# Expert units of 32 rows on four 32-column tiles in a mixture-of-experts stage

## What is computed

```python
def moe_ffn(h, w_router, b_router, w_gate_up, b_gate_up, w_down, b_down):
    ...
    top_logit, top_idx = lax.top_k(logits, TOP_K)      # 4 of 32 experts for each of 512 tokens
    top_w = jax.nn.softmax(top_logit, axis=-1)
    ...
    def expert_block(args):
        xe, e = args
        gu = xe @ w_gate_up[e] + b_gate_up[e]          # 1024 -> 2048
        gate = jnp.minimum(gu[:, :D_FF], SWIGLU_LIMIT)
        up = jnp.clip(gu[:, D_FF:], -SWIGLU_LIMIT, SWIGLU_LIMIT)
        act = (up + 1.0) * gate * jax.nn.sigmoid(SWIGLU_ALPHA * gate)
        return act @ w_down[e] + b_down[e]             # 1024 -> 1024
```

## Time and profile before

| | |
|---|---|
| time, 3 runs | 3245.38 us median, 3240.45 to 3245.57 |
| profiled execution | 3247.26 us, its span 3245.4 us |
| TensorE busy | 3111.7 us, 96% of the span |
| VectorE, ScalarE, GpSimd busy | 1361.0, 806.4, 388.4 us |
| granted TensorE clock, mean | 0.989 |
| moved by DMA | 632.90 MB |

### The profile page before, as it was taken

One profiled execution on the slowest core, in us unless ns is written; L12 is line 12 of the kernel. 1 busy time (PEld: TensorE's weight loads), 2 busy tenths in 40 slices (PEclk: granted clock), 3 DMA queues, 4 the chain that ended last, 5 costly groups with the idle time before them and its releaser, 6 DMA issues.

```text
span 3245.4 us, 41103 instructions
## 1 busy us (share of the span) xinstructions
PE 3111.7 (96%) x14106; PEld 1838.5 (57%) x14107; DVE 1361.0 (42%) x2096; ACT 806.4 (25%) x1573; POOL 388.4 (12%) x314
## 2 busy tenths in 40 slices
PE   7999899989999999999999999999999999999999
PEld 5555555464788633333333333333787888888887
DVE  2475555664345412121212121212467577554542
ACT  3343343420211211111111111111325355311100
POOL 0132221331000000000000000000301354000000
PEclk9999999999999999999999999999899999999999
DMA  5313142236312599999999997797412121222121
GB/s 222 117 72 130 59 143 97 98 152 229 128 52 106 203 348 394 381 386 383 389 393 388 380 390 279 304 364 275 154 52 95 59 72 49 88 91 78 65 78 56
DMA packets 190025, 632.90 MB, mean 195 GB/s; under 512 B 18752, under 2 KB 56000, under 8 KB 179168
## 3 DMA queue, kind: packets, MB, share of 16 engines
q1 hardware_dynamic: 161216, 552.79, 44.5%
q0 software_dynamic: 10944, 39.85, 3.4%
q10 hardware_dynamic: 17760, 38.78, 3.4%
HBM read 594.78 MB, written 36.57 MB: 195 GB/s over the span
## 4 chain that ended last, share of the span: by engine, by line
PE 78%; issue 7%; DMA 5%; DVE 4%; POOL 2%; ACT 2%; SPq 1%; ACTq 0%; DVEq 0%; POOLq 0%
PE ps L323 24%; PE ps L2325 17%; PE ps L2299 11%; PE ps L2016 7%; PE ps L272 6%; DMA slot<-in_w_exp 5%; PE ps L2554 2%; PE ps L2068 1%; POOL decay L3409 1%; PE ps L2526 1%; PE ps L2509 1%; PE ps L2294 1%; SPq L1358 1%; POOL x_dt L3398 1%; PE ps L1945 1%
## 5 line engine op out<-in xcount | busy, mean ns | idle before, releaser
L2325 PE MATMUL ps<-slot,xT_blk 128*64 128x512 f32 x3200 | 736.1, 601 | 28.7 <-DMA slot<-in_w_exp 26.4
L2325 PEld LDWEIGHTS ps<-slot,xT_blk 128*64 128x64 f32 x3200 | 219.0, 137 | 466.7 <-issue 378.0
L2299 PE MATMUL ps<-slot,aT 128*64 128x512 f32 x1632 | 362.8, 597 | 0.9 <-ACT aT L1706 0.9
L2016 PE MATMUL ps<-hT,slot 128*128 128x512 f32 (+1 forms) x896 | 309.5, 504 | 7.4 <-DVE xT L2734 6.3
L3065 DVE TENSOR_TENSOR gate<-ps,b_row 128x512 f32<-128x512 f32 x50 | 34.5, 691 | 520.2 <-PE ps L2325 520.1
L2299 PEld LDWEIGHTS ps<-slot,aT 128*64 128x64 f32 x1632 | 117.4, 137 | 237.9 <-issue 237.9
L2016 PEld LDWEIGHTS ps<-hT,slot 128*128 128x128 f32 x896 | 169.0, 191 | 136.7 <-issue 121.2
L2684 DVE SCALAR_TENSOR_TENSOR conv<-ps,g_conv,conv 128x510 f32<-128x510 f32 (+1 forms) x224 | 133.3, 631 | 178.5 <-ACT conv L1500 175.1
L3061 DVE MEMSET b_there<- 128x1 f32 x50 | 3.0, 59 | 386.5 <-DMA b_few<-in_b_gu 379.2
L1681 ACT ACTIVATE y_row<-ps 128x512 f32<-128x512 f32 x51 | 30.4, 597 | 383.9 <-PE ps L2299 383.9
L323 PE MATMUL ps<-in_t,in_s 128*128 128x264 f32 x528 | 124.8, 386 | 0.5 <-issue 0.5
(11 more groups left out here) (510 smaller groups left out, 4688.0 us busy)
## 6 DMA issues: line engine op xcount, KB each, us to landing
slot<-in_w_exp SPq DMA_DIRECT2D x768, 512.0 KB, 9.1
in_w<-in_w_ffn SPq DMA_DIRECT2D x22, 1024.0 KB, 4.8
expert_rows<-zero SPq DMA_DIRECT2D x4, 4608.0 KB, 22.4
slot<-in_w_xbc SPq DMA_DIRECT2D x8, 2048.0 KB, 7.7
sum_here<-sum_rows ACTq DMA_DIRECT2D x32, 512.0 KB, 3.6
w_modT<-in_w_modT POOLq DMA_DIRECT2D x32, 512.0 KB, 3.6
rnn_w<-in_w_rnn SPq DMA_DIRECT2D x16, 1024.0 KB, 4.8
expert_rows<-y_row ACTq DMA_DIRECT2D x102, 128.0 KB, 5.6
```

Of the source, the lines that this page charges most:

```text
L2016: last = pe.matmul(ps[:, 2 * (m % 2) + part, 0:n], w[:, (k * 4 + m % 4) * P:(k * 4 + m % 4 + 1) * P], hT[:, k, c0:c0 + n], start=(k == 0), ...
L2299: last = pe.matmul(ps[h * UNIT:(h + 1) * UNIT, 6, :], aT[:, t, d * UNIT:(d + 1) * UNIT], slot[4 + d][:, t * D + h * 512:t * D + (h + 1) * ...
L2325: last = pe.matmul(ps[h * UNIT:(h + 1) * UNIT, 2 * s + t, :], xT_blk[:, k, s * UNIT:(s + 1) * UNIT], slot[i // 4][:, at:at + 512], start=( ...
```

## The change

`UNIT` goes from 64 to 32 rows. A unit's stationary operand has 32 columns and stands on four 32-column tiles of the array. A gate/up piece still has 1024 columns of weights; its two matmuls over 512 columns go to two of the four tiles (pieces with an even number to tiles 0 and 1, the odd ones to 2 and 3), and the host lays the columns out for this. So a tile holds 256 gate and 256 up columns, the products take one PSUM bank where they took two, and the tiles of the activation are 128 x 256 where they were 128 x 512. A down piece takes four matmuls over 256 columns where it took two over 512. Loops run over four units of 32 rows (a quad) where they ran over two of 64. `turn_act` has two transposes where it had four, and it and the down product stand later (`TURN_AT, DOWN_AT` 6, 8 in place of 5, 6). Output rows of a unit are stored in four DMAs where there were two. The 24 places of the weights, their loads and what these wait for stay.

An expert is heavy now with more than two units. With the numbers of rows above it comes to 78 units of 32 rows: in the order of `turn_of`, 8 light experts have one unit, 8 light ones two, 12 heavy ones three, 2 four (109 and 128 rows) and 2 five (130 and 155 rows). The loop runs over 20 quads, so 80 units are worked through, two of them empty.

```diff
-UNIT = 64
+UNIT = 32
+TILES = P // UNIT
+PART = D // TILES
...
-    TURN_AT, DOWN_AT = 5, 6
+    TURN_AT, DOWN_AT = 6, 8
...
-        for h in range(2):
-            act.dma_start(expert_rows[bass.ds(u * UNIT, UNIT), h * 512:(h + 1) * 512], y_row[h * UNIT:(h + 1) * UNIT, :]).then_inc(s_yrow, 16)
+        for j in range(TILES):
+            act.dma_start(expert_rows[bass.ds(u * UNIT, UNIT), j * PART:(j + 1) * PART], y_row[j * UNIT:(j + 1) * UNIT, :]).then_inc(s_yrow, 16)
...
-        def down(d, t):
-            for h in range(2):
-                last = pe.matmul(ps[h * UNIT:(h + 1) * UNIT, 6, :], aT[:, t, d * UNIT:(d + 1) * UNIT],
-                                 slot[4 + d][:, t * D + h * 512:t * D + (h + 1) * 512],
-                                 start=(d == 0 and t == 0), stop=(d == 1 and t == 3))
+        def down(k):
+            tile, c = divmod(k, PART // P)
+            for j in range(TILES):
+                at = k % 4 * D + j * PART
+                last = pe.matmul(ps[j * UNIT:(j + 1) * UNIT, 6, 0:PART], aT[:, c, tile * UNIT:(tile + 1) * UNIT],
+                                 slot[4 + k // 4][:, at:at + PART], start=(k == 0), stop=(k == DN_PIECES - 1))
...
                         for h in range(2):
-                            at = i % 4 * PIECE + h * 512
-                            last = pe.matmul(ps[h * UNIT:(h + 1) * UNIT, 2 * s + t, :], xT_blk[:, k, s * UNIT:(s + 1) * UNIT],
+                            at, j = i % 4 * PIECE + h * 512, 2 * t + h
+                            last = pe.matmul(ps[j * UNIT:(j + 1) * UNIT, s % 2, :], xT_blk[:, k, s * UNIT:(s + 1) * UNIT],
                                              slot[i // 4][:, at:at + 512], start=(k == 0), stop=(k == KD - 1))
...
-        step("heavy", dve.tensor_scalar(heavy[:], n_of[:], 1.0, None, ALU.is_gt))
+        step("heavy", dve.tensor_scalar(heavy[:], n_of[:], 2.0, None, ALU.is_gt))
```

More of the change, by code:

```diff
@@ L136 @@
 CST = Columns([("ident", P), ("ones", P), ("le", P), ("gt", P), ("ge", P), ("lt", P),
-               ("expert", NE), ("odd", NE), ("unit", TABLE), ("filled", SEQ // UNIT), ("eps", 1), ("one", 1),
-               ("spot", P), ("pair", PAIR_TABLE + 1), ("token", SEQ // P), ("context", 2)])
+               ("expert", NE), ("odd", NE), ("filled", SEQ // UNIT), ("eps", 1), ("one", 1),
+               ("spot", P), ("quad", QUAD_TABLE + 1), ("token", SEQ // P), ("context", 2)])
 PRM = Columns([("c", 2 * KD), ("b_mod", 2 * N_MOD * KD), ("norm1", KD), ("norm2", KD), ("final", KD),
@@ L919, in program @@
     xT_blk = area("xT_blk", [P, KD, P])
-    y_row = area("y_row", [P, 512])
+    y_row = area("y_row", [P, PART])
     area = Area(AFTER_ROUTE, AFTER_SMALL + KD * SEQ * 4)
-    b_row = area("b_row", [P, 2, 512])
+    b_row = area("b_row", [P, 2, PART])
     area = Area(AFTER_X1)
[L924 to L927, removed]
+    gate = [area(f"gate{s}", [P, PART]) for s in range(2)]
+    up = [area(f"up{s}", [P, PART]) for s in range(2)]
+    sig = [area(f"sig{s}", [P, PART]) for s in range(2)]
+    aT = area("aT", [P, PART // P, P])
     area = Area(AFTER_X1 + 36 * 1024)
-    b_few = area("b_few", [P, 2, 512])
+    b_few = area("b_few", [P, 2, PART])
     b_there = area("b_there", [P, 1])
@@ L1689, in _ @@
         with act.Fori(0, n) as i:
-            for s in range(2):
-                u = i * 2 + s
+            for s in range(TILES):
+                u = i * TILES + s
+                last_unit = s == TILES - 1
                 act.wait_ge(moe_pe.sem, moe_pe.at("aT", u))
-                moe_act.done(act.activation(aT[:].rearrange("p t c -> p (t c)"), ps[:, 5, :], ACT.Copy), "aT")
+                moe_act.done(act.activation(aT[:].rearrange("p t c -> p (t c)"), ps[:, 5, 0:PART], ACT.Copy), "aT")
                 act.wait_ge(moe_pe.sem, moe_pe.at(f"dn{DN_PIECES - 1}", u))
                 moe_act.done(take_y(u), "y")
-                if s:
+                if last_unit:
                     take_xT(0, i)
@@ L2345, in _ @@
                 pe.wait_ge(moe_act.sem, moe_act.before("y", u))
[L2346 to L2349, removed]
-                gate_up(range(DOWN_AT, 8))
-                if s:
+                for k in range(DN_PIECES):
+                    pe.wait_ge(exp_loaded[GU_PIECES + k], e_before * 16 + 16)
+                    moe_pe.done(down(k), f"dn{k}")
+                if last_unit:
                     turn_x(0)
@@ L2354, in _ @@
                     pe.wait_ge(moe_xT_act.sem, moe_xT_act.before("half1", i))
-                gate_up(range(8, GU_PIECES))
-                if s:
+                gate_up(range(DOWN_AT, GU_PIECES))
+                if last_unit:
                     turn_x(1)
-        pe.wait_ge(moe_dve.sem, moe_dve.before("act", n * 2))
+        pe.wait_ge(moe_dve.sem, moe_dve.before("act", n * TILES))
         end_pe.done(turn_act(1), "aT")
         pe.wait_ge(end_act.sem, end_act.at("aT"))
-        pe.wait_ge(moe_act.sem, moe_act.before("y", n * 2))
-        for d in range(2):
-            for t in range(4):
-                pe.wait_ge(exp_loaded[GU_PIECES + 4 * d + t], 16 * NE)
-                last = down(d, t)
+        pe.wait_ge(moe_act.sem, moe_act.before("y", n * TILES))
+        for k in range(DN_PIECES):
+            pe.wait_ge(exp_loaded[GU_PIECES + k], 16 * NE)
+            last = down(k)
         end_pe.done(last, "down")
```

120 lines of the change are left out of this document (59 added, 61 removed).

## The result

The changed kernel takes **3325.84 us** (median of four runs, 3315.53 to 3330.79), the kernel before 3245.48 in the same job: a ratio of 1.0246, 95% interval 1.0223 to 1.027. The prediction was 3343, so its direction is right and its loss of 98 us is 18 us too large. The profiled execution of the changed kernel is the fastest of its four (3315.53 us, span 3313.7). Against that of before (3247.3) it is 68 us longer, where the medians differ by 80; in which part of the program the other executions lose their 8 to 15 us no trace shows.

The account below looks back on a forecast made before the run. Loads bound the expert stage and stand at heavy experts until the last unit releases places: 94 us more there (1259 against 1165.6) plus 4 us elsewhere on 3245 gives about 3343 us, range 3288 to 3420.

Parts of the forecast that it names:

- What bounds the stage, and that it stands still for want of places: Expert stage: loads bound it; they stop at heavy experts until the last unit frees places, 6.1 us at three units.
- 10.6 and 14.5 us: Three-unit heavy expert, after gu15 lands: down product follows down pieces to 10.6 us; third unit uses gu0 at 14.5.
- TensorE's unit of 10.9 us: TensorE, expert stage: gate/up 6.9, down product 3.4, transposes 0.4 and seams 0.2 us make 10.9 us a unit.
- 74.0 us for a pair: Expert stage: a light expert and a heavy one of three units take 67.9 us of loads plus 6.1 standing.
- The standing: Load stream at a three-unit heavy expert: stops for 6.1 us until gu0's place is refilled.
- Each further unit of an expert adds 11.2 us: Heavy experts beyond three units: 11.2 us more per unit, all standing; pairs take 85.2 us with four, 96.4 with five.
- Routing nothing, and 4 us for the rest: Outside the main stage sum: router table changes cancel at 0.3 us each way; remaining small delays add 4 us.
- the 0.2 us for each dense unit: Heavy experts, units behind the second: 0.2 us allowed each for a late sigmoid on ScalarE.
- first rival: Expert stage: places filled in time, loads keep 388 GB/s, stage 1110 us, 55 less, kernel 3190 us; chance 0.06.
- TensorE as the bound: Expert stage: TensorE's work sets the time, 896 us and some 15, kernel 2990 us; chance 0.02.
- The clock did fall: Expert stage: TensorE's clock falls after load waits, adding 54 us at heavy experts, kernel 3397 us; chance 0.12.
- Tiles in pairs only: TensorE, expert stage: waits keep two pieces from running together, a unit takes 21 us, kernel 3780 us; chance 0.03.

Follow-up runs that it names:

- control: Changed kernel with TensorE reading constant weights from a fixed place, all experts using the first one's biases, all waits kept: 3330.28 us.
- free stream: Changed kernel with constant weights from a fixed place, first expert's biases, and loads waiting only for the previous expert's first unit: 3163.48 us.

## Why the prediction was right, point by point

**What bounds the stage, and that it stands still for want of places**: right, and shown. With the waits moved and nothing else (control against free stream) 167 us go. The rows of one expert have its 10.6 and 14.5 us within 0.4, and the stream is near zero (14 to 28 GB/s) for 7 to 7.5 us at experts of three units (9 in one), for 17 and 19.5 at those of four and for 28 at those of five (forecast 6, 17 and 28).

**TensorE's unit of 10.9 us**: right to the digit (10.90). Four matmuls on four tiles of 32 columns take 0.43 us together, and a down product, 64 matmuls of 256 columns, has 3.64 us in its record when nothing is waited for, against 3.4 in the sum. In a unit the pieces overlap at their ends, so the sum holds.

**The size: 74.0 us for a pair, measured 72.65.** Two terms were mis-sized, and that they mostly cancel is luck. The stream's rate was put at 388 GB/s, the mean of a stretch with a DMA share of 0.99. The same prediction had the right number in another row: a piece of 0.524 MB every 1.28 us is 410 GB/s, and that is what flows here between the holes (408) and throughout with the stream free (410). The 388 had short holes in it, such as this one beside the pace behind it, in the kernel before:

```profile
1306.00:1310.00 4.00, 4.00 (x22) 1.39 (x20) 0.00 (x0) 1.88 (x2) 0.00 (x0) 1.00 0.52 125
1310.00:1320.00 10.00, 10.00 (x50) 3.54 (x48) 3.52 (x6) 0.87 (x2) 0.00 (x0) 1.00 1.02 411
```

By 410, 26.35 MB take 64.3 us. The standing, in turn, was put at 6.1 us and costs 72.65 - 64.3 = 8.4. The hole itself is 7 to 7.5 us long, and the stream also takes time to run down and to fill up: from 1960 to 1962 us it moved 262 GB/s and from 1970 to 1975 337. Together the two terms make 1.3 us in each pair, 21 us in 16. The stage is 18 us shorter than the forecast's 1259.

**Each further unit of an expert adds 11.2 us**: 84.1 and 94.8 against 72.65, 11.5 and 10.6 more: right.

**Routing nothing, and 4 us for the rest**: the two steps of the router whose tables grew take 0.69 us each in place of 0.42, and those whose tables shrank 0.13 less each. The time behind the stage is 1.6 us shorter, ahead of it 5.5 shorter, which is more than the 4 us and was not foreseen. TensorE's waits for VectorE's activation before the transposes, those of its weight loads first (us in all, times, longest):

```profile
PEld ps L2296 <- DVE gate L3078: 56.9, 62, 2.2
...
PE ps L2296 <- DVE gate L3078: 2.9, 5, 2.0
```

The matmuls themselves wait only 2.9 us in the whole stage, and 2.0 of these are at its last unit; the weight loads overlap earlier matmuls. So of the 0.2 us for each dense unit nothing came: such a unit takes 10.90 us.

**Sums that don't add up in the prediction.** In its first rival 1059 and 46 us are 1105, not 1110, and its own pairs without standing give 1095. Its bounds come to 3285 and 3417, the range is given as 3288 to 3420. Neither moves the forecast.

**The rivals.** The stream keeping its pace would give 3163, not 3190, and didn't happen. TensorE as the bound lies lower still: 3053 with half of each piece. The clock did fall: in ten-microsecond stretches before seven heavy experts, all behind a light one of a single unit, it was granted at 0.50 to 0.53, that is 1.2 GHz, with TensorE busy 0.9 to 4.0 us of ten. The pairs of three heavy units with such a stretch are no longer (72.1 to 72.7, and 73.8 for the last, behind which comes an empty unit) than those without (72.4 to 73.9, all with a second light unit): the clock is down only while the loads set the pace, and in the holes looked at, where the stream stands and TensorE's speed counts, it is 1.00. The Trainium skill (TensorE: Matmul & The Clock Gate, HAM oscillation) is right that waiting for DMA brings the clock down. That it costs time is not seen in this execution. The three longer executions of the changed kernel do have a lower mean clock, 0.974 to 0.978 against 0.980; what that did in them stays open. Tiles in pairs only: no, four run per 0.43 us.

## What to carry to other kernels

With weights in single-buffered places, the time to the last use of a place bounds the transfers, not how much faster the engine has become: smaller units that each stream all weights make the last use later, and a kernel whose transfers are at 99% turns every such microsecond into run time. To size such a hole, take the rate from the spacing of single transfers and not from the mean of a stretch, and add the run-down and the fill-up. Before extra places are bought with branches or copies, price what the selecting costs: here branches cost 577 us where the places could give some 160, and a copy on an idle engine lost half of its gain again by holding up VectorE. And in a summary of waits, keep TensorE's weight loads (56.9 us here) apart from its matmuls (2.9 us).

## What the runs showed of the hardware

- **Branches on TensorE.** Three comparisons and their jumps over unit-long pieces of code cost 7.4 us for each unit in the mean (594.0 us for 80). The loop over the units also jumps back in the changed kernel, after every fourth unit, but shows no gap of over 0.3 us there. The Trainium skill (Runtime: NRT & Kernel Launch, Instruction fetch mechanics) says that a taken branch out of the prefetched window waits for its code to be fetched, which the gaps agree with; no run here tells fetching from comparing.
- **GpSimd's copy and VectorE exclude each other.** With none of the copies beside them the last three operations on SBUF took 294, 425 and 425 ns (59 units); where a copy ran (21 units) 1019, 1087 and 868 ns in the mean, longer by less than one copy of 1.07 us. The first one on SBUF met a copy in 8 units and took 572 ns there. The operations that read PSUM stayed at 425 and 414 ns. The Trainium skill (SBUF — State Buffer, SBUF: two separate sides) says that the two engines share a port pair as an exclusive lock; the rows agree, for the operation with one input too (294 ns alone, 1019 beside a copy).
- **The stream's pace** was 408 to 410 GB/s between its holes in every kernel with the whole pieces, with one 512 KB piece every 1.28 us, whatever TensorE's form. Pieces cut to rows of 2 KB flowed at 281 to 312 GB/s, with a DMA share of 0.87 to 0.94.
